# Context feed-forward placed right behind the last expert's scatter, gate products moved to a later stage, three start orders changed

## The chip, the cores and the metric

One core of a Trainium2 chip runs the whole program, one launch. The metric is device time in microseconds from the start to the end of that launch; the profile is one further execution, taken by the hardware profiler, whose rows are in microseconds from its first instruction.

## What is computed

Two transformer blocks in float32 over 256 tokens of width 1024, cut here to what the change touches.

```python
x = x + mix @ w_out[0]; x = x + swiglu(rmsnorm(x, g), wg, wu, wd)        # layer 0: dense, 3584 wide
x = x + attention(rmsnorm(x, attn_norm[1])) ...                          # layer 1
x = x + moe_swiglu(rmsnorm(x, g), router, ...)                           # 8 experts, top 2 of them per token
x = rmsnorm(x, final_norm)
# second block; modulation vectors from silu(c) @ w_ada, for x and for a context of 256 tokens
xs = ffn_half(x, ...);  cs = ffn_half(ctx, ...)                          # the same weights, 2816 wide
#   ffn_half: s + 0.5 * gate * rmsnorm(swiglu(modulate(rmsnorm(s), shift, scale)), g_post)
xs = xs + mod * rmsnorm(token_mixer(...)); xs = ffn_half(xs, ...)        # last: ff1
```

## The kernel before

Each engine has an order of its own, written out by hand in one function per engine (SyncE for loads, TensorE, GpSimd, ScalarE, VectorE); semaphores tie them. There is no planner. A name such as `rows_high` (ScalarE) and `rows_low` (VectorE) is the same step's part on each engine.

**Products of split numbers.** A float32 matrix is split in a high part (ScalarE copies it with rounding, `..._high`) and a low part (VectorE subtracts the high part from the original, `..._low`). A product is three products: high by high, high by low, low by high. A block of weights is 1024 by 512, loaded in two halves of 1 MB into `ringA` (two blocks deep), and split half by half into `As`, which has one buffer (`A_parts` L2258, `unit_high`, `unit_low`), or for projections into `ringH`/`As` and `ringL` (`weight_high` L1573, `weight_low` L2226). Down weights go through `ringB` into `Bs`. SyncE reloads a half of `ringA` in a feed-forward when its low part is made, in a projection when TensorE has used it.

**A feed-forward** (`feed`, L783 for TensorE, L1610 ACT, L2268 DVE) runs over blocks of 256 hidden columns, for two tiles of 128 tokens. Per block TensorE does gate and up products with the first weight half (24), turns the hidden values of the block before, does 24 with the second half, then the block before's 24 down products. ScalarE does per block: hidden high part, As half, silu of two tiles, As half, Bs; VectorE the low parts of these and the product of gate and up. The hooks `before`, `after`, `turns_free` put other work at the start or the end of a given block. ff0c is the context's feed-forward, ff0x that of x with the same weights behind it; 11 blocks each.

**The experts** (`expert`, L965 PE, L1737 ACT, L2378 DVE) work on at most 128 gathered rows, so one tile: 14 blocks each of 12 + 12 + 12 products, with the gather of the next expert's rows in block 12 and the scatter of the one before's result (`keep_y`, `y_low`, `scatter` L952, `add` L2367) in blocks 2 and 3. The last expert ends with its own order in the last block: an alternative home for the down weights (`down_home`), then three products of the identity that nothing reads (`idle_products` L701), then its two scatters, each followed by VectorE's add to x through the same two accumulator banks 6 and 7.

**Behind the experts**, before: VectorE signals x; ScalarE and VectorE split the context rows `hcT` into `xs` (`x_parts`); ScalarE takes the squares of x, VectorE scales it with the final norm, ScalarE takes each tile's statistics for ff0x's norm and VectorE scales into `xn` (L1937 to L1943, L2735 to L2746); then ff0c's loop starts. Its hooks turn the rows of ff0x (`x_rows`) in blocks 1 to 3 and split them into `hcTR` and `hTR`.

**The second attention's start** (L1788 ff., L2503 ff.): two weight halves are split, the dense result is added tile by tile (`settle`), each tile is normed (`tile_stats`, `tile_root`, `tile_scale`), turned by TensorE (`turn_rows`), and split (`rows_high`, `rows_low`).

**GpSimd** (L1469) does two things: it finishes the modulation columns, and after the last modulation row it forms four gate rows (L1487 to L1500) of 128 by 1024, with six loads of 0.5 MB on its own queue. The first reader of these is the end of ff0c (`post`, in ff0x's first block).

**ff1's start** (L2968 ff.): VectorE makes both As halves, then for tile 0 `mixed_out`, `mixed_add`, `tile_scale`, and so on.

Of the kernel before, what the change touches and what calls it, by code (L numbers as in the profile page):

```python
# [28 lines left out]
P = 128  # L29
SEQ = 256  # L30
D = 1024
# [101 lines left out]
def build(nc, t, out, AT1, N1, AT2, N2):  # L133
    ctx = ExitStack()
    with ctx:
# [14 lines left out]
        hcT = sb("hcT", [P, KC, SEQ])  # L150
        xn = sb("xn", [P, TILES, D])
# [113 lines left out]
        split_h = [hcTR, hTR]  # L265
        Kc, Vc = gateG[:, 0:2, :], cs
# [149 lines left out]
        for nm in ("attn0", "mix0", "ffn0", "attn1", "mix1", "ffn1", "ff0x", "ff1"):  # L416
            mixed, plain = nm[:3] == "mix", nm in ("ffn1", "ff0x")
            PN[nm] = dict(at, mixed=mixed, plain=plain)
            for key, add_ in (("std", 2), ("xn", 4 if mixed else 2), ("tp", 4), ("hi", 2 if plain else 4), ("lo", 2 if plain else 4)):
                at[key] += add_  # L420

# [275 lines left out]
        def _(pe):  # L697
# [24 lines left out]
            def turn_rows(nm, tt, hf):  # L722
# [3 lines left out]
                for j in range(4):  # L726
                    last = tr(ps[:, rows_bank(nm, tt, hf), j * P:(j + 1) * P], xn[:, tt, (4 * hf + j) * P:(4 * hf + j + 1) * P], ident)
# [224 lines left out]
            def scatter(e, tt):  # L952
# [5 lines left out]
                if tt or isinstance(e, int) and e == NE - 1:  # L958
                    pe.wait_ge(added, 2 * e + tt)
                for half in range(2):  # L960
                    for q in range(2):
                        last = mm(ps[:, 6 + half, :], selT[:, tt, :], ye[q][:, half * 512:(half + 1) * 512], start=q == 0, stop=q == 1)
# [176 lines left out]
            for l in range(2):  # L1139
# [17 lines left out]
                if l == 0:  # L1157
                    feed(ph["dense"], split_stream, 2, rows="ffn0")
            def logits(tt):
# [26 lines left out]
            with pe.If(pe.value_load(most[0:1, 0:1], min_val=0, max_val=SEQ) < CAP + 1):  # L1186
# [5 lines left out]
                idle_products(3)  # L1192
# [12 lines left out]
            def x_rows_out(n):  # L1205

                if n in (2, 3):
                    pe.wait_ge(pn_hi, PN["ff0x"]["hi"] + n - 1)
                    pe.wait_ge(pn_lo, PN["ff0x"]["lo"] + n - 1)
            feed(ph["ff0c"], split_stream, 2, ready=2 * ph["ff0c"]["xc"] + 1, xsm=xs_split, head=2, drains=False, after=x_rows, turns_free=x_rows_out)  # L1210
            feed(ph["ff0x"], lambda l, tt, k: split_h[l][:, k, tt * P:(tt + 1) * P], 2, ready=2 * ph["ff0x"]["xc"] + 1, xsm=xs_split, leads=False)
# [258 lines left out]
        def _(pool):  # L1470
# [16 lines left out]
            pool.wait_ge(spread_copied, units_before(NADA))  # L1487
            for w, (gain, bias, rows_, fac) in enumerate(((1, 2, (0, 1), 0.5), (3, 5, (2,), 1.0), (5, 8, (3,), 0.5))):
# [15 lines left out]
        def _(act):  # L1504
# [39 lines left out]
            def tile_stats(nm, tt, src, wait, cols=None, j=None):  # L1544
# [5 lines left out]
                ch.done(A(xn[:, tt, sl], src[:, tt, sl], ACT.Square, accum_out=ss[:, j:j + 1]))  # L1550
# [174 lines left out]

            def rows_part(e, h):
# [10 lines left out]
            def expert(e):  # L1737
# [3 lines left out]
                def before(n):  # L1741
                    if n == 2 and not first:
                        keep_y(e - 1)

                def body(i, u, last):
# [4 lines left out]
                    if not lead:  # L1750
                        part_high(e, i - 1, u, 1)
                    unit_high(e, *nxt, 0)
# [7 lines left out]
                    if last and final:  # L1760
# [1286 lines left out]
```

## Time and profile before

| | us |
|---|---|
| three runs | 2671.5, 2678.55, 2677.37 |
| their median | 2677.37 |
| the profiled execution's own time | 2677.7 |
| its span, first to last instruction | 2675.9 |
| PE busy (mean granted clock 0.975 of full speed) | 2551.6 |
| DVE busy | 1824.0 |
| ACT busy | 1452.0 |
| POOL busy | 57.5 |

PE is TensorE, DVE VectorE, ACT ScalarE, POOL GpSimd, SP SyncE (SPq its queue of loads). A row of a timeline has start, duration of the group, engine, line, operation, tiles written and read, shape and count; in brackets how long the engine was idle before it and what ended that. A PE matmul row's duration includes the pipeline's drain, so starts are better compared than ends. The chain of waits is the work that ended last, followed back from the end; its rows have start, duration, engine, tile written, line and count.

### The profile page before, as it was taken

Reading aid. Unit: us, or ns where it says so; the run is one execution under the profiler, and the core shown is the slowest. Engines: PE = TensorE matmul, PEld = TensorE weight load, DVE = VectorE, ACT = ScalarE, POOL = GpSimd, SP = SyncE. Lnnn points to the kernel's source line nnn. Section 1 sums busy time; section 2 is a strip of 40 time slices with the busy share of each in tenths; the row PEclk is TensorE's granted clock in tenths of the full one; section 3 lists DMA queues with packets and bytes.
Section 4 is the critical chain, followed back from the end, with each engine's and each line's share of the span. In section 5 each row is a group of like instructions: output and inputs, shape, how many; then the busy total and the mean of one; then the engine's idle time right before and its main releaser. Section 6 shows DMA issues by size and latency. Waiting matters only on the chain.

```text
span 2675.9 us, 33561 instructions
## 1 busy us (share of the span) xinstructions
PE 2551.6 (95%) x11949; PEld 2028.0 (76%) x11949; DVE 1824.0 (68%) x1779; ACT 1452.0 (54%) x1613; POOL 57.5 (2%) x40
## 2 busy tenths in 40 slices
PE   7899998888999999999999998999999999998998
PEld 6578887666878787888888886888884687776787
DVE  6554555559898989888888886555443475776544
ACT  4554434545777777777777675445432343465443
POOL 0000000016000000000000000000000000000000
PEclk9989998889999999999999998999999999999999
DMA  6865542758999999999999996556543344435552
GB/s 216 294 215 186 184 169 79 252 181 328 356 348 349 353 342 358 348 351 349 353 340 361 332 345 217 180 182 194 181 166 108 99 148 119 137 100 175 195 185 70
DMA packets 327742, 631.65 MB, mean 236 GB/s; under 512 B 14088, under 2 KB 112936, under 8 KB 327464
## 3 DMA queue, kind: packets, MB, share of 16 engines
q1 hardware_dynamic: 326792, 627.35, 67.5%
q0 software_dynamic: 864, 3.15, 0.3%
q8 instruction: 55, 0.90, 0.1%
q14 instruction: 31, 0.25, 0.0%
HBM read 629.40 MB, written 1.05 MB: 236 GB/s over the span
## 4 chain that ended last, share of the span: by engine, by line
PE 84%; DVE 8%; ACT 4%; issue 3%; DMA 1%; SPq 0%; DVEq 0%; ACTq 0%
PE ps L894 18%; PE ps L820 18%; PE ps L924 11%; PE ps L849 9%; PE ps L1289 6%; PE ps L754 5%; PE ps L1316 2%; PE ps L1221 2%; DVE As L2261 2%; PE ps L1027 1%; PE ps L949 1%; ACT As L1679 1%; PE ps L833 1%; PE ps L909 1%; PE ps L1280 1%
## 5 line engine op out<-in xcount | busy, mean ns | idle before, releaser
L2261 DVE TENSOR_TENSOR As<-ringA,As 128x2048 fp32r<-128x2048 f32 x318 | 737.8, 2322 | 220.2 <-ACT As L1598 127.5
L894 PE MATMUL ps<-As,xgs 128*128 128x512 f32 x2688 | 660.9, 395 | 10.5 <-DVE As L2261 7.8
L894 PEld LDWEIGHTS ps<-As,xgs 128*128 128x128 f32 x2688 | 494.9, 188 | 117.6 <-DVE As L2261 6.8
L1679 ACT ACTIVATE As<-ringA 128x2048 fp32r<-128x2048 f32 x224 | 428.7, 1914 | 29.9 <-PE ps L894 28.1
L820 PE MATMUL ps<-As,xs 128*128 128x512 f32 x1632 | 391.5, 396 | 9.3 <-DVE xs L2199 5.3
L820 PEld LDWEIGHTS ps<-As,xs 128*128 128x128 f32 x1632 | 305.8, 189 | 76.1 <-issue 5.7
L924 PE MATMUL ps<-Bs,hds 128*128 128x512 f32 x1332 | 324.6, 393 | 13.7 <-DVE hds L2322 13.5
L924 PEld LDWEIGHTS ps<-Bs,hds 128*128 128x128 f32 x1332 | 250.0, 189 | 72.5 <-issue 19.3
L2341 DVE TENSOR_TENSOR Bs<-ringB,Bs 128x2048 fp32r<-128x2048 f32 x111 | 260.4, 2346 | 11.0 <-ACT Bs L1709 9.5
L1709 ACT ACTIVATE Bs<-ringB 128x2048 fp32r<-128x2048 f32 x111 | 213.1, 1920 | 74.8 <-PE ps L924 74.8
L849 PE MATMUL ps<-Bs,hds 128*128 128x512 f32 x1056 | 247.8, 390 | 0.0
L849 PEld LDWEIGHTS ps<-Bs,hds 128*128 128x128 f32 x1056 | 198.0, 188 | 41.9
L1598 ACT ACTIVATE As<-ringA 128x2048 fp32r<-128x2048 f32 x94 | 179.8, 1913 | 16.7 <-DMA ringA<-in_dense_w_up 9.7
L2305 DVE TENSOR_TENSOR Bs<-ringB,Bs 128x2048 fp32r<-128x2048 f32 x44 | 100.9, 2293 | 119.7 <-ACT Bs L1652 119.7
L1652 ACT ACTIVATE Bs<-ringB 128x2048 fp32r<-128x2048 f32 x44 | 84.3, 1916 | 135.4 <-PE ps L849 135.4
L2231 DVE TENSOR_TENSOR ringL<-ringA,ringH 128x2048 fp32r<-128x2048 f32 x42 | 96.1, 2290 | 57.3 <-ACT ringH L1578 57.1
L1689 ACT ACTIVATE hds<-ps 128x256 fp32r<-128x256 f32 x112 | 43.0, 384 | 156.2 <-PE ps L909 155.5
L754 PE MATMUL ps<-As,xs 128*128 128x512 f32 (+1 forms) x384 | 119.0, 393 | 8.6 <-DVE ringL L2231 5.7
L1619 ACT ACTIVATE hds<-ps 128x256 fp32r<-128x256 f32 x94 | 31.3, 382 | 171.1 <-PE ps L833 163.1
L1578 ACT ACTIVATE ringH<-ringA 128x2048 fp32r<-128x2048 f32 x42 | 80.1, 1911 | 79.1 <-PE ps L1289 57.6
L820 PE MATMUL ps<-As,hcTR 128*128 128x512 f32 x352 | 111.6, 398 | 0.0
L1640 ACT ACTIVATE sg<-ps 128x256 f32<-128x256 f32 x94 | 36.0, 383 | 126.1 <-PE ps L820 125.1
(380 smaller groups left out, 3210.2 us busy)
## 6 DMA issues: line engine op xcount, KB each, us to landing
ringA<-in_moe_w_gate SPq DMA_DIRECT2D x112, 1024.0 KB, 5.1
ringA<-in_moe_w_up SPq DMA_DIRECT2D x112, 1024.0 KB, 5.7
ringB<-in_moe_w_down SPq DMA_DIRECT2D x112, 1024.0 KB, 5.5
ringA<-in_w_ff_in SPq DMA_DIRECT2D x132, 512.0 KB, 4.8
ringA<-in_w_in SPq DMA_DIRECT2D x56, 1024.0 KB, 5.4
ringA<-in_w_ada SPq DMA_DIRECT2D x36, 1024.0 KB, 6.2
ringB<-in_w_ff_out SPq DMA_DIRECT2D x33, 1024.0 KB, 5.0
ringA<-in_dense_w_gate SPq DMA_DIRECT2D x28, 512.0 KB, 3.6
```

The lines of the kernel that those rows point to most:

```text
L754: m = mm(ps[:, 4 + 2 * (n % 2) + tt, 0:cols], xs[:, l, k, tt * P:(tt + 1) * P], w, start=k == 0 and m_ == 0, stop=k == KC - 1 and m_ == 2)
L820: m = mm(ps[:, bank, :], lhs(l, tt, k), As[:, h, r, k % 4, :], start=k == 0 and n == 0, stop=k == KC - 1 and n == 2)
L849: m = mm(ps[:, 4 + 2 * tt + half, :], hds[:, buf, l, q, :], w[:, half * 512:(half + 1) * 512], start=first and q == 0 and n == 0, stop=q = ...
L894: m = mm(ps[:, bank, :], lhs(l, tt, k), As[:, h, r, k % 4, :], start=k == 0 and n == 0, stop=k == KC - 1 and n == 2)
L924: m = mm(ps[:, 4 + 2 * tt + half, :], hds[:, u if T == 1 else tt, l, q, :], (Bs[:, q, r, :] if weights is None else weights[r][:, q, :])[: ...
L1289: m = mm(dst, lhs[l][:, k, tt * P:(tt + 1) * P], w[q], start=k == 0 and m_ == 0, stop=k == KC - 1 and m_ == 2)
L1598: A(As[:, h, 0, :, :], ringA[:, (p["a"] + u) % 2, 4 * h:4 * h + 4, :], ACT.Copy).then_inc(A_high, 1)
L1679: A(As[:, h, 0, :, :], ringA[:, (p["a"] + u) % 2, 4 * h:4 * h + 4, :], ACT.Copy).then_inc(A_high, 1)
L1709: A(Bs[:, :, 0, :] if dst is None else dst, ringB[:, b0 % 2, :, :], ACT.Copy).then_inc(B_high, 1)
L2261: V.tensor_tensor(As[:, h, 1, :, :], ringA[:, (p["a"] + u) % 2, 4 * h:4 * h + 4, :], f32(As[:, h, 0, :, :]), ALU.subtract).then_inc(A_spli ...
L2305: V.tensor_tensor(Bs[:, :, 1, :], ringB[:, (p["b"] + u) % 2, :, :], f32(Bs[:, :, 0, :]), ALU.subtract).then_inc(B_low, 1)
L2341: V.tensor_tensor(lo, ringB[:, (p["b"] + u) % 2, :, :], f32(hi), ALU.subtract).then_inc(B_low, 1)
```

## The change

1. The gate rows on GpSimd wait until the second of ff0x's row turns is through (`pn_lo`), in ff0c's third block.
2. The context rows are split in blocks 0 and 1 of the last expert, into `xn` and `hcTR` (`context_high`, `context_low`), once its own gather has read `xn`.
3. The last expert's last block has a new order on ACT and DVE: down weights and the product of gate and up before ff0c's first As halves, the second of which comes after the accumulator is saved. The two scatters use banks 6, 7 and 2, 3, so the second does not wait for the first one's add; two idle products instead of three.
4. The squares of x, its final norm and ff0x's statistics move into ff0c: on ACT to the start of block 1, ahead of the hidden parts, with a table load behind; on DVE to the end of block 0. They use an area of the arena (`x_tok`) instead of `xn`; `tokens(nm)` gives that area to the helpers `tile_stats`, `tile_scale` and `turn_rows`. ff0x's rows are split into `xs` and `hTR` (`split_x`).
5. Two idle products behind the dense feed-forward; at the second attention's start DVE adds tile 0 before its first weight half and makes the second half after tile 0's rows; ACT copies the second half after tile 0's root and turns to tile 1's square after tile 0's rows.
6. At ff1's start DVE makes the second As half after tile 0's add.

The diff, cut; the numbers are lines of the kernel before, indentation is one blank per level, `xnR` is `xn` seen as rounded numbers.

```diff
@@ -263 @@
   split_h = [hcTR, hTR]
+  split_c = [xnR[:, :, :].rearrange("p t n -> p (t n)").rearrange("p (k n) -> p k n", k=KC), hcTR]
+  split_x = [xs[:, 1, :, :], hTR]
+  x_tok = ar(0, TILES, D)
@@ -418 @@
+  def tokens(nm):
...
+   return x_tok if nm == "ff0x" else xn[:, :, :]
@@ -955 @@
       pe.wait_ge(xg_ready, 2 * e + 4)
-    if tt or isinstance(e, int) and e == NE - 1:
+    final = isinstance(e, int) and e == NE - 1
+    if final != bool(tt):
      pe.wait_ge(added, 2 * e + tt)
+    bank = 2 if final and tt else 6
...
      for q in range(2):
-      last = mm(ps[:, 6 + half, :], selT[:, tt, :], ye[q][:, half * 512:(half + 1) * 512], start=q == 0, stop=q == 1)
+      last = mm(ps[:, bank + half, :], selT[:, tt, :], ye[q][:, half * 512:(half + 1) * 512], start=q == 0, stop=q == 1)
@@ -1156 @@
      feed(ph["dense"], split_stream, 2, rows="ffn0")
+     idle_products(2)
@@ -1189 @@
     expert(NE - 1)
-    idle_products(3)
+    idle_products(2)
@@ -1204 @@
+    if n == 1:
+     pe.wait_ge(x_ready, XR["moe"])
...
      pe.wait_ge(pn_lo, PN["ff0x"]["lo"] + n - 1)
-   feed(ph["ff0c"], split_stream, 2, ready=2 * ph["ff0c"]["xc"] + 1, xsm=xs_split, head=2, drains=False, after=x_rows, turns_free=x_rows_out)
-   feed(ph["ff0x"], lambda l, tt, k: split_h[l][:, k, tt * P:(tt + 1) * P], 2, ready=2 * ph["ff0x"]["xc"] + 1, xsm=xs_split, leads=False)
+   feed(ph["ff0c"], lambda l, tt, k: split_c[l][:, k, tt * P:(tt + 1) * P], 2, ready=2 * ph["ff0c"]["xc"] + 1, xsm=xs_split, head=2, drains=False, after=x_rows, turns_free=x_rows_out)
+   feed(ph["ff0x"], lambda l, tt, k: split_x[l][:, k, tt * P:(tt + 1) * P], 2, ready=2 * ph["ff0x"]["xc"] + 1, xsm=xs_split, leads=False)
@@ -1485 @@
    pool.wait_ge(spread_copied, units_before(NADA))
+   pool.wait_ge(pn_lo, PN["ff0x"]["lo"] + 2)
@@ -1723 @@
+   def context_high(h):
...
+    act.wait_ge(nt_act, 4 * (call["ff0c"] + 1))
+    act.wait_ge(nt_dve, 4 * (call["ff0c"] + 1))
+    A(split_c[0][:, 4 * h:4 * h + 4, :], hcT[:, 4 * h:4 * h + 4, :], ACT.Copy).then_inc(xs_high, 1)
@@ -1739 @@
     def before(n):
+     if n == 0 and final:
+      act.wait_ge(gathered, 2 * NE)
+     if n in (0, 1) and final:
+      context_high(n)
@@ -1749 @@
       part_high(e, i - 1, u, 1)
+     if last and final:
+      down_high(e, i, 0, down_home(ph["moe"], ph["moe"]["b"])[0], 0)
+      unit_high(e, *nxt, 0)
+      part_high(e, i, 0, 1)
+      part_high(e, i, 1, 1, 3)
+      down_high(e, i, 1, None, 2)
+      unit_high(e, *nxt, 1)
+      return
@@ -1757 @@
       rows_part(e + 1, 1)
-     if last and final:
-      down_high(e, i, 0, down_home(ph["moe"], ph["moe"]["b"])[0], 0)
-      part_high(e, i, 0, 1)
-      part_high(e, i, 1, 1, 3)
-      down_high(e, i, 1, None, 2)
-     elif u:
+     if u:
@@ -1795 @@
      act.wait_ge(tile_done, p["td"])
-     for h in range(2):
-      weight_high(p, 0, h)
+     weight_high(p, 0, 0)
...
      tile_root(tt, tt + 1, D)
-     if tt == 0 or l == 0:
-      continue
-     for hf in range(2):
-      rows_high(f"attn{l}", 0, hf, col(8 * l))
+     if l and tt == 0:
+      weight_high(p, 0, 1)
+      for hf in range(2):
+       rows_high(f"attn{l}", 0, hf, col(8 * l))
@@ -1934 @@
     all_tokens(NE - 1)
-   act.wait_ge(x_ready, XR["moe"])
-   x_parts(hcT, call["ff0c"])
...
-   squares(lambda tt: x[:, tt, :], 1, 1e-5)
-   for tt in range(TILES):
-    tile_stats("ff0x", tt, x, [(x_ready, XR["final"])])
-    tile_root(tt, tt + 1, D, 1e-6)
+    for h in range(2):
+     context_high(h)
@@ -1949 @@
+    if n == 1:
+     act.wait_ge(x_ready, XR["moe"])
+     squares(lambda tt: x[:, tt, :], 1, 1e-5, lambda tt, q: x_tok[:, tt, :])
+     for tt in range(TILES):
+      tile_stats("ff0x", tt, x, [(x_ready, XR["final"])])
+      tile_root(tt, tt + 1, D, 1e-6)
+     nc.scalar.preload_act_table(ACT.Silu)
@@ -1960 @@
      for h in range(2):
-      A(hcTR[:, 4 * h:4 * h + 4, :], hT[:, 4 * h:4 * h + 4, :], ACT.Copy).then_inc(xs_high, 1)
+      A(split_x[0][:, 4 * h:4 * h + 4, :], hT[:, 4 * h:4 * h + 4, :], ACT.Copy).then_inc(xs_high, 1)
@@ -2367 @@
     dve.wait_ge(mixed_back, 2 * e + (tt + 1))
-    V.tensor_tensor(x[:, tt, :], x[:, tt, :], ps[:, 6:8, :].rearrange("p a b -> p (a b)"), ALU.add).then_inc(added, 1)
+    b = 2 if tt and isinstance(e, int) and e == NE - 1 else 6
+    V.tensor_tensor(x[:, tt, :], x[:, tt, :], ps[:, b:b + 2, :].rearrange("p a b -> p (a b)"), ALU.add).then_inc(added, 1)
@@ -2380 @@
     def after(n):
+     if n in (0, 1) and final:
+      context_low(n)
@@ -2401 @@
       part_low(e, i - 1, u, 1)
+     if last and final:
+      gate_times_up(e, i, 1)
+      down_low(e, i, 0, down_home(ph["moe"], ph["moe"]["b"]))
+      part_low(e, i, 0, 1)
+      part_low(e, i, 1, 1, 3)
+      down_low(e, i, 1)
+      unit_low(e, *nxt, 0)
+      y_low(e)
+      unit_low(e, *nxt, 1)
+      return
@@ -2409 @@
       rows_part(e + 1, 1)
-     if last and final:
-      down_low(e, i, 0, down_home(ph["moe"], ph["moe"]["b"]))
-      part_low(e, i, 0, 1)
-      part_low(e, i, 1, 1, 3)
-      down_low(e, i, 1)
-     elif u:
+     if u:
@@ -2422 @@
     if final:
-     y_low(e)
...
+   def context_low(h):
...
+    dve.wait_ge(xs_high, 2 * ph["ff0c"]["xc"] + h + 1)
+    V.tensor_tensor(hcTR[:, 4 * h:4 * h + 4, :], hcT[:, 4 * h:4 * h + 4, :], f32(split_c[0][:, 4 * h:4 * h + 4, :]), ALU.subtract).then_inc(xs_split, 1)
@@ -2508 @@
     else:
+     settle(0)
      weight_low(p, 0, 0)
-     settle(0)
-     weight_low(p, 0, 1)
...
       rows_low(attn, 0, hf, col(8 * l))
+     weight_low(p, 0, 1)
@@ -2732 @@
     dve.wait_ge(acc_free, 1 + NE)
+    for h in range(2):
+     context_low(h)
    dve.sem_inc(x_ready, 1)
-   x_parts(hcT, ph["ff0c"]["xc"])
...
-   dve.wait_ge(nrm_std, SQ["final"])
-   ch.done(V.reciprocal(rr[:, 0:2], std[:, 0:2]))
-   for tt in range(TILES):
-    last = V.scalar_tensor_tensor(x[:, tt, :], x[:, tt, :], rr[:, tt:tt + 1], fnrow[:, :], ALU.mult, ALU.mult)
-   last.then_inc(x_ready, 1)
-   dve.wait_ge(x_ready, XR["final"])
-   for tt in range(TILES):
-    tile_scale("ff0x", tt, x, tt + 1)
...
+    if n == 0:
+     dve.wait_ge(nrm_std, SQ["final"])
+     ch.done(V.reciprocal(rr[:, 0:2], std[:, 0:2]))
+     for tt in range(TILES):
+      last = V.scalar_tensor_tensor(x[:, tt, :], x[:, tt, :], rr[:, tt:tt + 1], fnrow[:, :], ALU.mult, ALU.mult)
+     last.then_inc(x_ready, 1)
+     dve.wait_ge(x_ready, XR["final"])
+     for tt in range(TILES):
+      tile_scale("ff0x", tt, x, tt + 1)
@@ -2755 @@
       dve.wait_ge(xs_high, 2 * ph["ff0x"]["xc"] + h + 1)
-      V.tensor_tensor(hTR[:, 4 * h:4 * h + 4, :], hT[:, 4 * h:4 * h + 4, :], f32(hcTR[:, 4 * h:4 * h + 4, :]), ALU.subtract).then_inc(xs_split, 1)
+      V.tensor_tensor(hTR[:, 4 * h:4 * h + 4, :], hT[:, 4 * h:4 * h + 4, :], f32(split_x[0][:, 4 * h:4 * h + 4, :]), ALU.subtract).then_inc(xs_split, 1)
@@ -2968 @@
     weight_low(p, 1, h)
-   for h in range(2):
-    A_parts(ph["ff1"], 0, 0, 0, h)
+   A_parts(ph["ff1"], 0, 0, 0, 0)
@@ -3002 @@
    mixed_add(0)
+   A_parts(ph["ff1"], 0, 0, 0, 1)
```

## Rows read from the trace of the kernel before

**Rows 1.** The page, part 4: shares of the chain that ended last.

```profile
PE 84%; DVE 8%; ACT 4%; issue 3%; DMA 1%; SPq 0%; DVEq 0%; ACTq 0%
```

**Rows 2.** Windows: length, busy PE, PEld, DVE, ACT, POOL (counts), PEclk, DMA share, GB/s.

```profile
594.00:724.00 130.00, 115.53 (x513) 92.90 (x512) 113.53 (x68) 82.33 (x60) 46.30 (x18) 0.97 0.93 340
724.00:850.00 126.00, 124.44 (x574) 101.84 (x573) 111.52 (x81) 89.71 (x67) 0.00 (x0) 1.00 0.97 350
1670.00:1740.00 70.00, 70.00 (x324) 57.86 (x322) 38.28 (x38) 33.04 (x39) 0.00 (x0) 1.00 0.56 181
```

**Rows 3.** The chain from 408 to 428 us: start, us, engine, tile, line, count.

```profile
410.10 2.30 DVE ringL L2231
415.84 0.75 DVE xn L2207
417.75 1.16 ACT xn L1550 x2
419.23 1.04 ACT xs L1563 x4
420.29 1.14 DVE xs L2223 x4
421.56 5.46 PE ps L754 x12
427.02 1.30 PE ps L727 x8
```

**Rows 4.** First expert: timeline of POOL and DVE, then PE's waits from 594 to 665.

```profile
601.48 7.32 POOL L1493 TENSOR_TENSOR gateG<-gateG,arow 128x1024 f32<-128x1024 f32 x2 [5.21 <-DMA arow<-in_b_ada]
602.08 8.88 DVE L2261 TENSOR_TENSOR As<-ringA,As 128x2048 fp32r<-128x2048 f32 x2
609.71 7.35 POOL L1496 TENSOR_SCALAR gateG<-gateG 128x1024 f32<-128x1024 f32 x2
612.14 2.29 DVE L2261 TENSOR_TENSOR As<-ringA,As 128x2048 fp32r<-128x2048 f32 x1 [1.19 <-ACT As L1679]
...
PE ps L894 <- DVE As L2261: 7.8, 6, 2.1
PE ps L924 <- DVE hds L2322: 5.1, 3, 3.0
```

**Rows 5.** Experts to ff0c: page part 6, timeline, and two chain rows.

```profile
ringB<-in_moe_w_down SPq DMA_DIRECT2D x112, 1024.0 KB, 5.5
...
1610.10 0.37 SPq L604 DMA_DIRECT2D ringB<-in_moe_w_down  x1
...
1617.28 1.90 ACT L1709 ACTIVATE Bs<-ringB 128x2048 fp32r<-128x2048 f32 x1
...
1619.74 1.22 PE L924 MATMUL ps<-hTR,hds 128*128 128x512 f32 x2 [2.86 <-DVE hds L2322]
...
1638.58 1.04 ACT L1514 ACTIVATE xn<-x 128x1024 f32<-128x1024 f32 x1
...
1639.95 12.37 PE L820 MATMUL ps<-As,xs 128*128 128x512 f32 x47 [5.32 <-DVE xs L2199]
...
1640.91 1.28 ACT L1515 ACT_TABLE_LOAD   x1
...
1647.81 0.30 ACT L1554 ACTIVATE std<-ss,small 128x1 f32<-128x1 f32 x1
...
1628.34 2.58 PE ps L704 x6
...
1664.35 5.46 PE ps L849 x24
```

**Rows 6.** A middle expert's block 2, timeline of PE.

```profile
884.56 3.01 PE L924 MATMUL ps<-Bs,hds 128*128 128x512 f32 x12 [0.28 <-DVE hds L2322]
```

**Rows 7.** Groups by form, PE: 1700 to 1784 (ff0c), 1840 to 1925 (ff0x).

```profile
L820 PE MATMUL ps<-As,xs 128*128 128x512 f32 x240 | 57.1, 394 | 0.0
...
L820 PE MATMUL ps<-As,hcTR 128*128 128x512 f32 x160 | 50.7, 398 | 0.0
```

More of the change, by code:

```diff
@@ L150, in build @@
         hcT = sb("hcT", [P, KC, SEQ])
+        with nc.sbuf_tensor("xnR", [P, TILES, D], F32R) as xnR:
+            pass
         xn = sb("xn", [P, TILES, D])
@@ L726, in turn_rows @@
                 for j in range(4):
-                    last = tr(ps[:, rows_bank(nm, tt, hf), j * P:(j + 1) * P], xn[:, tt, (4 * hf + j) * P:(4 * hf + j + 1) * P], ident)
+                    last = tr(ps[:, rows_bank(nm, tt, hf), j * P:(j + 1) * P], tokens(nm)[:, tt, (4 * hf + j) * P:(4 * hf + j + 1) * P], ident)
                 last.then_inc(pn_tp, 1)
@@ L1549, in tile_stats @@
                 sl = slice(0, D) if cols is None else cols
-                ch.done(A(xn[:, tt, sl], src[:, tt, sl], ACT.Square, accum_out=ss[:, j:j + 1]))
+                ch.done(A(tokens(nm)[:, tt, sl], src[:, tt, sl], ACT.Square, accum_out=ss[:, j:j + 1]))
             def tile_root(j0, j1, n, eps=1e-5):
@@ L2206, in tile_scale @@
                 ch.done(V.reciprocal(rr[:, j:j + 1], std[:, j:j + 1]))
-                V.tensor_scalar(xn[:, tt, sl], src[:, tt, sl], rr[:, j:j + 1], None, ALU.mult).then_inc(pn_xn, 1)
+                V.tensor_scalar(tokens(nm)[:, tt, sl], src[:, tt, sl], rr[:, j:j + 1], None, ALU.mult).then_inc(pn_xn, 1)
             def rows_low(nm, tt, hf, scale):
```

## The prediction

> **What bounds the kernel now.** I read the page's chain first: of the work that ended last TensorE (PE) holds 84%, VectorE (DVE) 8% and ScalarE (ACT) 4% [rows 1]. So time is won only where PE stands idle or runs at 1.2 GHz. The windows say where that is [rows 2]: in the first expert PE is idle 130.0 - 115.5 = 14.5 us at a granted clock of 0.97, in the next one 1.6 us at 1.00; in the context feed-forward (ff0c) PE is busy 70.0 of 70.0 us with DVE at 38.3. The change touches four seams (dense to second attention, first expert, experts to ff0c, start of ff1), and I step through each with the durations of the rows. The sum is made against the profiled execution's own 2677.7 us (span 2675.9), 0.3 us above the median of the runs shown, 2677.37.
>
> **1. Start of the second attention: 5.5 us earlier.** The chain before [rows 3] runs: ACT copies a half weight, DVE subtracts it (410.10, 2.30), only then adds the dense result, subtracts the second half, scales tile 0; ACT does tile 1's square (417.75) before tile 0's rows (419.23, 1.04), DVE their low half (1.14), and PE starts at 421.56. After: DVE adds tile 0 while ACT copies, so ACT squares at about 410.3 and DVE subtracts one half meanwhile, 410.3 to 412.6. Scaling takes 0.75 and 0.2 around it: 413.5. Half the transposes 0.7, ACT 1.04, DVE 1.14: first product at 416.7, 4.9 earlier. PE then wants tile 1: DVE finishes tile 0's other rows (417.7), the moved subtraction (2.30, 420.0) and the scale (0.9): transposes at 421.0 in place of 427.02, 6.0 earlier. The two idle products are 0.9 each by the three of [rows 5] (2.58 for x6): they fill 411.9 to 413.7, just before the transposes, and cost at most 0.2. The twelve products that took 5.46 (1.2 GHz; 24 warm ones take 5.46 too, [rows 5]) may stay at 2.4 GHz, as the gaps are then under 2 us; if not, they end at 422.2 and the gain is 4.8. I take 5.5, ends 3 and 6.5. Weight loads of this seam are issued when PE frees a half and shift with it.
>
> **2. Gate products out of the first expert: 11 us.** POOL works 46.3 us there [rows 2]. While it runs a two-input product (601.48) two DVE subtractions take 8.88 together, against 2.29 each otherwise, 4.3 more; beside its one-input product (609.71) one takes 2.29 [rows 4]. PE waits 7.8 us for As subtractions and 5.1 for hidden ones there, 12.9 of its 14.5 idle. Part of that stays: with 2.29 a subtraction, 1.9 a copy and 2.75 for twelve products [rows 5], the one As buffer leaves waits of 1.5, 0.6, 0.8 and 0.1 in the first two blocks, and the one-hots about 1.0 in block 3: 4.0 in all. The low clock goes too, 3% of 130 us is 3.9 us of full speed, of which I count 2 because PE was idle for the rest. 12.9 - 4.0 + 2 = 11. Ends: 8 (clock gives nothing and a wait is left), 13.
>
> The products now follow the second turn of ff0x's rows, so POOL and its six 0.5 MB loads lie in ff0c. DVE is busy 38.3 of 70 us there and PE never waits [rows 2]; even the 4.3 of a pair is under the 7.7 us that DVE has free in each block of 16.9 (three groups of 24 products at 5.5 and a turn). Cost 0, other end 3. Their reader, the end of ff0c, is over 100 us later. Without that cover the cost is rival 3.
>
> A rule speaks against this. The rows: DVE at 2.29 beside POOL's one-input product. The Trainium skill, "SBUF — State Buffer", section on SBUF's two sides, says that VectorE with two SBUF inputs and GpSimd take the shared port pair for a whole instruction and the loser blocks. The two-input rows agree, the one-input row does not. By that rule every subtraction in ff0c could wait for one POOL instruction (3.7 us) and the sum would be 11.4 in place of 23.4, a time of 2666; by the row it is 2654.
>
> **3. Experts to ff0c: 8.4 us earlier.** Before [rows 5]: PE waits 2.86 and starts the last two blocks' down products at 1619.74 at the low clock; three idle products (2.58); scatter, add, scatter; x split into xs; 5.32 idle; ff0c from 1639.95. After, step by step. Two As subtractions (2 x 2.29) leave DVE's queue ahead of the down weights: down starts at 1615.1. Twelve products, 1617.8. The last down block's copy started at 1617.28 behind ACT's other work; its load was issued at 1610.1 and takes 5 to 5.5, so about 1615.4; a copy of 1.9 and a subtraction of 2.3 later PE goes on at 1619.7, done 1622.4. Accumulator copied (1.1, like the square of that size) and subtracted (1.2, half of 2.29), with handovers 2.5; two scatters without the add between (own banks), 1.9: 1626.9. The context rows are split already, so ff0c's first product is there, 13 us earlier; its second As half is due at 1632.4 and ready at 1627.2. 48 products: 1637.9; 24, turn, 24: 1649.4. Now the new wait: ACT, once its Bs copy ends (1642.2), does the final norm's squares and ff0x's statistics before the hidden copies. That stretch ran from 1638.58 to 1648.11 [rows 5], and a table load of 1.28 more makes it 10.8: 1653.0, hidden parts 0.9, down products at 1653.9 in place of 1664.35: 10.4 earlier. Behind ACT's stretch stand its As and Bs copies, which PE reaches later than they need. The 4.5 idle lowers the clock, as 5.32 did (47 products in 12.37 in place of 10.8): minus 2.0. 8.4. Ends 5 and 11. DVE's part of that norm lies inside the stretch.
>
> **4. Context split in the last expert: 2.0 us lost.** DVE is busy 111.5 of 126 [rows 2] and gets two more subtractions of half size (1.2 each by the 2.29 one) in blocks 0 and 1. ACT has room. DVE's slack is 14.5 of 126, about 1.0 a block; behind the second stand the y subtraction and the hidden one that PE already waited 0.28 for at that place [rows 6]: 2.4 + 0.28 less the 0.7 that blocks 0 and 1 can absorb beside their own unevenness gives 2.0, ends 0.5 and 3.
>
> **5. Operands.** ff0c reads xn and hcTR in place of xs, ff0x reads xs and hTR in place of hcTR and hTR. A product is 394 ns from xs, 398 from hcTR [rows 7]; 528 products in each stage at 4 ns are 2.1 us, lost in one and won in the other: 0, ends -2 and +2.
>
> **6. ff1: 0.5 us.** The second As subtraction (2.29, [rows 4]) stood before tile 0's mix and now stands after its add, beside ACT's square; it delays the scale by 0.8 of the 1.4 that it frees. Loads wait for that half but SP is still issuing others.
>
> Sum: 5.5 + 11 + 8.4 - 2.0 + 0 + 0.5 = 23.4; 2677.7 - 23.4 = 2654.
>
> **Rivals.** *Forecast*, 0.64: about 2654, own range 2647 to 2661.
> *1, the final norm eats the seam*, 0.14: ACT's stretch in ff0c's second block grows to twice its 10.8 less what PE has to do meanwhile, and PE goes slow for longer; item 3 gives 1 to 2: 2661. For it: a chain over ACT and DVE in the middle of PE work. Against: its parts lasted 9.5 together.
> *2, the first expert is paced by loads*, 0.08: that window moved 340 GB/s at a share of 0.93, the next 350 at 0.97 [rows 2]. The same bytes in 119 us want 371. At 355 the window would need 124.5: item 2 gives 5.5: 2660. Against: no wait of PE's there leads back to a load.
> *3, the gate products cost as much in ff0c*, 0.08: three subtractions a block, each behind a 3.7 us POOL instruction, take 18 us, with DVE's smaller parts about 20.6, 3.7 over a block's 16.9; POOL's 46.3 us of work last for three to four blocks: 12 us back, 2666. It is the port rule of the Trainium skill's "SBUF — State Buffer" told above.
> *4, slower*, 0.03: ff0c's stationary halves lie in two tensors (xn, hcTR) and each of its 528 products loses time in the weight load. To end over 2677.4 + 8 it must take 31 us, 59 ns a product on 229. The rows know 4 ns, hence the small chance; anything under 44 ns still ends below before.
> *5, it does not do what it says*, 0.03: ff0c's first product still waits as it did, since the gathered path is not what decides but the late As half, and rivals 2 or 3 come along: 2670 to 2677.
>
> **How the numbers follow.** 2654 is the forecast case. The range of 2646 to 2665 takes nearly all of it and rivals 1 and 2; it leaves out about 2 in 10. A measurement of this kernel can tell about 0.3% (8 us) from no change. Faster by more: the forecast, rivals 1 and 2 and half of 3, 0.90. Within: the other half of 3 and rival 5, 0.07. Slower: rival 4, 0.03.
>
> **What would show it.** Right: no POOL row near 600 and As subtractions of 2.29 there; the second gather 11 us earlier relative to the first; POOL's rows some 35 us after ff0c's start with PE busy throughout; first attention product 5 us after the dense stage's last one and not 10; two scatters back to back, ff0c's products directly behind; one new wait of 4 to 5 us of PE's down products for hidden parts in ff0c's second block. Wrong: waits of PE for As or hds in ff0c's blocks 3 to 6 (rival 3), DMA as a releaser in the first expert (rival 2), a wait over 8 us in ff0c's second block (rival 1), a mean over 400 ns for ff0c's products (rival 4), or a wait over 3 us in the last expert's third block (item 4).

## The result and the profile after

| | before | after |
|---|---|---|
| median of the runs | 2677.96 (4 runs, 2671.5 to 2682.1) | 2656.01 (4 runs, 2654.8 to 2659.7) |
| the profiled execution | 2677.7 | 2659.7 |
| its span | 2675.9 | 2657.9 |
| PE busy, mean granted clock | 2551.6, 0.975 | 2548.6, 0.978 |

The ratio is 0.9918 with a 95% interval of 0.9895 to 0.9942: 22 us by the medians. The profiled execution of after is 3.7 above its median, so the two traces differ by 18.0 only. The change was run once more under the name after_again: 2657.17 (6 runs), span 2657.7.

The chain of the page of after, beside [rows 1]: PE gains a point, DVE loses one.

```profile
PE 85%; DVE 7%; ACT 4%; issue 3%; DMA 1%; SPq 0%; DVEq 0%; ACTq 0%
```

**A ledger by stages** comes from the starts of the same PE work in each trace; what is left over between two such marks is the stage's own. Gathers are the eight `ps<-arena,xn` groups; a turn in this table is a group of transposes of hidden values, `ps<-c,hh`.

| from, to (us) | before | after | item |
|---|---|---|---|
| dense's last down group to the attention's last projection | 64.2 | 57.9 | 1 |
| to the first gather | 118.9 | 117.2 | |
| first to second gather | 128.3 | 116.4 | 2 |
| second to last gather | 757.7 | 757.7 | |
| last gather to the last expert's first scatter | 150.5 | 146.3 | 3, 4 |
| to ff0c's first product | 9.1 | 3.9 | 3 |
| to ff0c's first down products | 24.2 | 28.7 | 3 |
| to the turn in ff0c's block 2 | 11.8 | 14.8 | 3 |
| to ff0x's last turn | 332.8 | 334.0 | 5 |
| to ff1's first turn | 490.1 | 492.3 | 6 |

Windows of after, columns as in [rows 2]: the first expert has no POOL, the next is as it was, and ff0c now carries POOL for 43.3 us with PE still busy all the time. POOL's first product starts 67 us behind ff0c's first one (1678.36 against 1611.25), where the prediction had said some 35.

```profile
587.00:703.00 116.00, 110.92 (x499) 90.35 (x498) 95.20 (x67) 81.11 (x59) 0.00 (x0) 0.98 0.94 346
703.00:829.00 126.00, 124.49 (x574) 101.90 (x573) 111.82 (x80) 89.66 (x66) 0.00 (x0) 1.00 0.98 353
1670.00:1740.00 70.00, 70.00 (x313) 57.00 (x312) 44.58 (x35) 29.71 (x30) 43.26 (x18) 1.00 0.71 226
```

The chain of after at the second attention's start, beside [rows 3]: the dense stage's end, the idle products (L713), tile 0's turn, rows, and the first products at 417.15.

```profile
404.12 8.26 PE ps L858 x36
412.39 1.72 PE ps L713 x4
...
417.15 4.51 PE ps L763 x12
421.67 0.87 PE ps L736 x8
```

Experts to ff0c, beside [rows 5]. Timeline of PE and ACT of after, with the idle time ahead in brackets.

```profile
1601.81 2.97 PE L933 MATMUL ps<-Bs,hds 128*128 128x512 f32 x12 [1.44 <-DVE Bs L2370]
1607.30 0.50 PE L973 MATMUL ps<-arenaR 128*128 128x512 f32 x1 [0.81 <-DVE hTR L2478]
1609.03 0.39 PE L973 MATMUL ps<-hTR,arenaR 128*128 128x512 f32 x1
1611.25 0.82 PE L829 MATMUL ps<-As,xnR 128*128 128x512 f32 x2 [1.83 <-issue]
1618.73 1.92 ACT L1613 ACTIVATE As<-ringA 128x2048 fp32r<-128x2048 f32 x1 [12.80 <-PE ps L829]
1628.17 1.04 ACT L1529 ACTIVATE arena<-x 128x1024 f32<-128x1024 f32 x1
1634.84 1.06 ACT L1565 ACTIVATE arena<-x 128x1024 f32<-128x1024 f32 x1 [2.75 <-DVE x L2786]
1638.99 0.66 ACT L1634 ACTIVATE hds<-ps 128x256 fp32r<-128x256 f32 x2
1639.94 8.46 PE L858 MATMUL ps<-Bs,hds 128*128 128x512 f32 x24 [4.07 <-issue]
```

The scatters are back to back and ff0c starts 2.2 us behind the last of them. Its first down products wait 4.07 us: their releaser reads "issue", but ACT's hidden copies end at 1639.65 and DVE's low parts follow, and ahead of them on ACT stands the norm from 1628.17 to 1638.98. The trace also shows a hole that the prediction had not seen: ACT idle for 12.80 us up to 1618.73, right where x is complete.

### The profile page after: what moved, and what is told of

Read it like the earlier page. It is cut to its first block, busy times and chain, and to the rows that moved or that the text cites. A ratio compares the mean times of both kernels' runs of the same rounds, so it can differ in the third digit from the quotient of the medians.

```text
span 2657.9 us, 33567 instructions
## 1 busy us (share of the span) xinstructions
PE 2548.6 (96%) x11951; PEld 2023.4 (76%) x11951; DVE 1814.3 (68%) x1779; ACT 1452.1 (55%) x1613; POOL 54.4 (2%) x40
## 4 chain that ended last, share of the span: by engine, by line
PE 85%; DVE 7%; ACT 4%; issue 3%; DMA 1%; SPq 0%; DVEq 0%; ACTq 0%
PE ps L829 19%; PE ps L903 19%; PE ps L933 11%; PE ps L858 10%; PE ps L1303 6%; PE ps L763 5%; PE ps L1330 2%; PE ps L1235 1%; DVE As L2290 1%; PE ps L1038 1%; PE ps L958 1%; PE ps L918 1%; PE ps L842 1%; ACT Bs L1724 1%; ACT As L1694 1%
## 5 line engine op out<-in xcount | busy, mean ns | idle before, releaser
L829 PE MATMUL ps<-As,xs 128*128 128x512 f32 x1456 | 376.1, 396 | 3.9 <-DVE hh L2325 3.9
L933 PE MATMUL ps<-Bs,hds 128*128 128x512 f32 x1332 | 322.4, 391 | 11.8 <-DVE hds L2351 9.0
L829 PEld LDWEIGHTS ps<-As,xs 128*128 128x128 f32 x1456 | 271.9, 189 | 63.3 <-DVE hh L2325 4.8
L2370 DVE TENSOR_TENSOR Bs<-ringB,Bs 128x2048 fp32r<-128x2048 f32 x111 | 254.1, 2290 | 12.4 <-ACT Bs L1724 10.8
L1613 ACT ACTIVATE As<-ringA 128x2048 fp32r<-128x2048 f32 x94 | 179.8, 1913 | 29.1 <-PE ps L829 12.8
L829 PE MATMUL ps<-As,xnR 128*128 128x512 f32 x352 | 112.8, 402 | 1.8 <-issue 1.8
```

The lines of the kernel that those rows point to most:

```text
L829: m = mm(ps[:, bank, :], lhs(l, tt, k), As[:, h, r, k % 4, :], start=k == 0 and n == 0, stop=k == KC - 1 and n == 2)
L933: m = mm(ps[:, 4 + 2 * tt + half, :], hds[:, u if T == 1 else tt, l, q, :], (Bs[:, q, r, :] if weights is None else weights[r][:, q, :])[: ...
L1613: A(As[:, h, 0, :, :], ringA[:, (p["a"] + u) % 2, 4 * h:4 * h + 4, :], ACT.Copy).then_inc(A_high, 1)
L2370: V.tensor_tensor(lo, ringB[:, (p["b"] + u) % 2, :, :], f32(hi), ALU.subtract).then_inc(B_low, 1)
```

## The experiments

Medians below stand beside 2656 to 2657 for the changed kernel. A single trace says less than it seems to: with the same code ahead of it, the dense stage's last down group starts anywhere from 406.6 to 411.9 us. So stages are compared, and a stage with its clock beside it.

**1. The gate products alone**, on the kernel before.

```diff
     pool.wait_ge(spread_copied, units_before(NADA))
+    pool.wait_ge(pn_lo, PN["ff0x"]["lo"] + 2)
```

> The kernel before with one edit: the four gate rows on POOL wait for the second of ff0x's row turns. The traces of before and after put the two gathers around the first expert 128.1 and 116.2 us apart, 11.9 less. Theory (POOL's two-input products slow the subtractions there, and they cost nothing in ff0c): 11 to 12 us under before, the same 11.9 between the gathers, and DVE subtractions of 4 us and more beside POOL's two-input rows in ff0c with no wait of PE's behind them. Rival (the change's other edits made the first expert shorter, its starting clock above all): under 6 us. Rival (they cost as much in ff0c): within 2 us of before.

Measured: 2665.74 (6 runs) against 2679.06, ratio 0.9943 (0.9923 to 0.9964). Gather to gather 114.9 in place of 128.3, 13.4 less; from the turn in block 2 to ff0x's last one 332.8 as before, so in ff0c the products cost nothing. The theory holds. 1.5 more than 11.9 is the clock of the first gather: its products lead to the first expert's own in 5.7 us here, and in 7.2 in before and in after.

**2. The gate products back**, in the changed kernel (the same line taken out).

> The changed kernel with the gate rows back in the first expert. Theory: 11 to 12 us over the changed kernel, all of it between the first two gathers (116.2 back to 128). Rival (they cost 3 us or more in ff0c): the first expert loses 12, and ff0c from its 25th product on gets 3 or more shorter, 9 or less over the changed kernel.

Measured: 2673.16 (12 runs), 17 over the changed kernel, and 134.1 between the gathers: 17.6 lost, not 11.9. From ff0c's block 2 on it is 334.0 as in after, so rival 3 is out to the hundredth. The same work costs 11.9 to 13.4 in one timing and 17.6 in another. Between the gathers PE stands idle 17.2 us here, 14.5 in before and 5.1 in after; the rest of the difference to before is clock, granted at 0.93 here and at 0.97 in before. PE's waits here, from 586 to 721, against 7.8 and 5.1 of [rows 4]:

```profile
PE ps L903 <- DVE As L2289: 10.3, 5, 4.1
PE ps L933 <- DVE hds L2350: 5.5, 1, 5.5
```

**3. Gate products of one input**, in the first expert.

```diff
-     ch.done(G.tensor_tensor(gateG[:, g, :], gateG[:, g, :], vec_row, ALU.add))
+     ch.done(G.tensor_scalar(gateG[:, g, :], gateG[:, g, :], 0.5, None, ALU.mult))
```

and the same for the product with the gain.

> The changed kernel with the gate rows back in the first expert, and every product and sum of two tiles on POOL there put in as a product of one tile and a constant, so the gate rows are not the reference's: the same six loads and 12 instructions of 128 by 1024 on POOL, none with two inputs. The first two gathers lie 116.4 us apart without POOL's work and 134.1 with it. Theory (it is POOL's two-input instructions that hold up DVE's subtractions): DVE's subtractions stay at 2.3 us beside POOL, 116.4 to 118 between the gathers. Rival (any POOL instruction blocks DVE's two-input ones for as long as it runs, the port rule): the POOL work is as long or longer, so 134 or more. Rival (the six loads of 0.5 MB in the way of the weights): 120 or more with DVE at 2.3.

Measured: 2660.78 (5 runs); 119.4 between the gathers, 2.9 over no POOL work and 14.7 under two-input work. The window shows POOL as busy as with two inputs (44.2 us), and the first instructions of DVE beside it:

```profile
593.32 6.42 POOL L1507 TENSOR_SCALAR gateG<-gateG 128x1024 f32<-128x1024 f32 x2 [5.25 <-DMA arow<-in_b_ada]
594.82 2.28 DVE L2289 TENSOR_TENSOR As<-ringA,As 128x2048 fp32r<-128x2048 f32 x1
598.46 2.29 DVE L2289 TENSOR_TENSOR As<-ringA,As 128x2048 fp32r<-128x2048 f32 x1 [1.36 <-ACT As L1693]
```

In the run with two inputs the same two came out as one pair of 7.48:

```profile
593.19 5.15 POOL L1507 TENSOR_TENSOR gateG<-gateG,arow 128x1024 f32<-128x1024 f32 x2 [5.16 <-DMA arow<-in_b_ada]
596.05 7.48 DVE L2289 TENSOR_TENSOR As<-ringA,As 128x2048 fp32r<-128x2048 f32 x2
```

DVE's mean As subtraction from 586 to 660 is 2.46 us against 3.09, with 2.29 undisturbed. Of the sixteen subtractions of 128 by 2048 that overlap a one-input row eleven took 2.3 and five 3.0 to 3.45, the longest this one beside the POOL row at 651.28:

```profile
651.28 2.79 POOL L1510 TENSOR_SCALAR gateG<-gateG 128x1024 f32<-128x1024 f32 x1
651.03 5.66 DVE L2289 TENSOR_TENSOR As<-ringA,As 128x2048 fp32r<-128x2048 f32 x2
```

(its pair is 3.45 and 2.28). So it is mostly the two-input instructions; a small price, 2.9 us, is left, and whether the loads or those longer rows make it stays open. By the port rule of the Trainium skill's "SBUF — State Buffer" every one of POOL's instructions would have held DVE's; the rows agree for two inputs and not for one. Nor are one-input rows free of DVE: POOL's own took 2.79 us at best and up to 4.43 beside it.

**4. The second attention's start back** in the changed kernel (the orders of ACT and DVE as before, no idle products).

> The changed kernel with the start of the second attention as before: both weight halves ahead, no idle products behind the dense feed-forward. Theory: 6.3 us lost up to the seam's end and the heads' 1.6 with it, so 6 to 8 over the changed kernel, PE's first attention product 10 us behind the dense feed-forward. Rival (the 1.6 in the heads was chance): 6.3 at the seam and nothing more behind it.

Measured: 2663.48 (6 runs), 7 over by the medians and 10.0 by the trace. To the last projection it is 63.6 against 57.9, 5.7 of it; the other 4.3 arises in the heads. The granted clock of the 30 us behind the projection goes with it (windows of after, then of this run):

```profile
469.30:499.30 30.00, 26.46 (x214) 16.70 (x213) 19.36 (x38) 14.63 (x51) 0.00 (x0) 1.00 0.86 297
```

```profile
475.07:505.07 30.00, 26.83 (x182) 16.45 (x184) 17.82 (x33) 13.60 (x47) 0.00 (x0) 0.83 0.77 266
```

Dense's last down group to the first gather took 175.1 to 176.2 us in ten of eleven traces with the new order and 183.1, 185.2 and 185.0 in the three with the old one. The eleventh, of experiment 6, has the new order, took 179.5, and has a clock of 0.83 there. So the theory's 6.3 + 1.6 is not what happens: the same code behind the seam runs at one of several clocks, 0.83, 0.94 or 1.00, and two of these came with either order. With the old order it never had the best, but that is three traces, and whether the order bears on it is not shown.

**5. No idle products behind dense.**

```diff
-     idle_products(2)
```

> The changed kernel without the two idle products behind the dense feed-forward. They were to keep PE at 2.4 GHz for the first attention products and did not: the first eight or so of twelve still ran at 1.2. Theory (they do nothing here): the transposes behind them and the first attention product, 5.39 us after the dense stage's last down group, come within 0.3 us of that, and the twelve products take the same 4.5. Rival (they did keep a part of the clock): the eight transposes take 2 us in place of 1.1 and the twelve products 5.3, 1 to 2 us later on.

Measured (one run, 2654.68): the first attention product 5.38 behind the last down group, against 5.39, at the same cold start:

```profile
408.82 1.09 PE L736 MATMUL ps<-c,xn 128*128 128x128 f32 x8 [1.62 <-DVE xn L2235]
411.96 0.76 PE L763 MATMUL ps<-As,xs 128*128 128x512 f32 x1 [2.05 <-DVE xs L2251]
```

The idle products do nothing here: with them and without them PE stands 2.05 us ahead of the first attention product and runs at 1.2 GHz for 3.4 us from there on.

**6. The norm in the hole.** On ACT the squares before block 0, the statistics behind its first As half; on DVE the scaling of x before the loop.

```diff
-    if n == 1:
+    if n == 0:
      act.wait_ge(x_ready, XR["moe"])
      squares(lambda tt: x[:, tt, :], 1, 1e-5, lambda tt, q: x_tok[:, tt, :])
...
+   def x_stats(n):
...
+   feed(ph["ff0c"], 2, ahead=True, head=2, drains=False, before=x_rows, mid=x_stats)
```

> The changed kernel with the final norm taken out of ACT's way: the squares of x and their root at the very start of ff0c, where ACT's trace is idle for 12.8 us and DVE's for 8.9; DVE scales x at once; ACT's statistics for ff0x follow its first As half in block 0, DVE's scaling of the rows its own. Theory (PE's 4.07 us before ff0c's first down products is ACT's norm ahead of the hidden copies, and the 24 products of 8.46 us after it are slow for that wait): the wait is gone, the 24 products take 5.5, 7 us under the changed kernel. Rival (the copies of block 0 come late instead, As for the next block or the first silu): a new wait of 1 to 4 us at the next As half and a gain of 3 or less. Rival (the wait has another cause, as PE's down weights): it stays, no change.

Measured: 2651.94 (6 runs), ratio 0.9898 (0.9880 to 0.9916). From ff0c's first product to its first down products 25.2 in place of 28.7, from there to block 2's turn 12.0 in place of 14.8: 6.3 less. The wait and the slow products after it are gone together, so the cause is ACT's norm. The size needs a range: seven other traces with after's code from ff0c on take 40.7 to 42.7 us for the two stretches together, against 43.5 in after and after_again, 37.1 here, so 3.6 to 6.3 less. A small part of the first rival is there too, silu behind the statistics:

```profile
PE ps L829 <- DVE hh L2333: 1.4, 1, 1.4
```

**7. The norm split.** Squares at the start with the scaling, the statistics in block 1 again.

```diff
-    if n == 1:
+    if n == 0:
      act.wait_ge(x_ready, XR["moe"])
      squares(lambda tt: x[:, tt, :], 1, 1e-5, lambda tt, q: x_tok[:, tt, :])
+    if n == 1:
      for tt in range(TILES):
...
+   feed(ph["ff0c"], ..., before=x_rows, mid=lambda n: nc.scalar.preload_act_table(ACT.Silu) if n == 0 else None)
```

> The changed kernel with only the squares of x and their root at the start of ff0c on ACT, DVE's scaling with the final norm right behind, ACT's silu table again behind its first As half; ACT's statistics for ff0x stay ahead of the hidden copies of block 1, DVE's scaling of the rows at the end of block 0. In the run that moved all of it, PE waited 1.4 us for the product of gate and up, whose silu stood behind the statistics. Theory (each piece fits in a gap of its own): ACT's stretch in block 1 is 5.5 us in place of 9.5 and starts at the same place, so the hidden parts are there 0.6 us before PE wants them and neither the 4.07 nor the 1.4 wait is left; 8 us under the changed kernel. Rival (the stretch in block 1 with its two table loads is still too long): a wait of 1 us or more before the first down products and no more than the 6.6 us that the whole move gave.

Measured: 2651.99 (6 runs, 2648.03 to 2656.65), profiled span 2646.2. 23.2 and 12.0 for the two stretches, 8.3 less than after and 5.5 to 7.6 less than the seven others: both waits are gone. Of the 11.7 us between the spans of this trace and after's, 5.1 lie ahead of the first seam, where the code is the same. Its PE waits and the down products:

```profile
1606.15 0.70 PE L829 MATMUL ps<-As,xnR 128*128 128x512 f32 x2 [1.60 <-issue]
1629.36 2.91 PE L858 MATMUL ps<-Bs,hds 128*128 128x512 f32 x12
1631.66 3.35 PE L858 MATMUL ps<-Bs,hds 128*128 128x512 f32 x14
```

The medians differ by 5.2 from after_again, at the lower end of that range, with ratios to before of 0.9916 (0.9900 to 0.9931) and 0.9929 (0.9915 to 0.9943): the stage is shown in the trace, its size in whole runs is not settled.

**8. Idle products behind the branch.**

```diff
      all_tokens(NE - 1)
+   idle_products(8)
```

> The changed kernel with eight idle products (some 1.9 us) right behind the branch that ends the experts on PE. PE stands 1.83 us between the last scatter product and ff0c's first one, with its operands ready. Theory (it is the way out of the branch): the gap of 1.8 stays ahead of the idle products, and ff0c's first product comes 1.9 later behind them. Rival (ff0c's first product waits for something that the profile does not show): the idle products follow the scatter at once and fill the gap, ff0c's first product stays where it was.

Measured (one run, 2661.35): the gap stays ahead of the idle products.

```profile
1609.26 7.13 PE L713 MATMUL ps<-c 128*128 128x512 f32 x16 [1.74 <-issue]
1615.83 1.03 PE L829 MATMUL ps<-As,xnR 128*128 128x512 f32 x2
```

They wait for no semaphore, so the 1.7 us is not a wait of ff0c's for its operands but belongs to leaving the branch, as the theory has it. The packets of the instruction queue say more: in all fourteen traces a load of 16 KB of instructions lands 1.4 to 1.5 us before PE issues its first instruction behind the branch. In after it runs from 1608.54 to 1609.72, with PE's next instruction at 1611.14; where it lands later behind the last scatter, the gap is longer, from 1.5 us up to 2.1. In before it runs from 1637.31 to 1638.44, with PE's next instruction at 1639.84, and xs's first half was ready at 1638.99, so the wait of 5.32 that [rows 5] puts down to xs may have ended by this load instead. That the load is the cause is read from these times alone; no run was made to move it.

The eight products took 7.1 us, not 1.9, and at full clock:

```profile
1609.30:1616.00 6.70, 6.70 (x17) 3.10 (x17) 0.64 (x1) 0.00 (x0) 0.00 (x0) 1.00 0.87 307
```

This window of PE, PEld, DVE, ACT and POOL has a granted clock of 1.00. One idle product is two instructions of 0.43 us each, as the three of [rows 5] were (2.58 for x6); eight are 6.9 by that row, so the expectation's 1.9 was mispriced. ff0c came 6.5 later behind the scatter. The way from its first product to its first down products, 27.5 us, is 1.2 shorter than in after, but five other traces without idle products take 27.2 to 27.8 as well: it is the clock of ff0c's start, not these products.

**9. One more DVE instruction ahead of each context half.**

```diff
+      ch.done(V.tensor_tensor(hcT[:, 4 * h:4 * h + 4, :], hcT[:, 4 * h:4 * h + 4, :], hcT[:, 4 * h:4 * h + 4, :], ALU.max))
```

> The changed kernel with one more DVE instruction of two inputs and 128 by 1024 ahead of each half of the context split in the last expert's blocks 0 and 1 (the larger of a tile and itself, which leaves it as it is). The context split moved the last expert's last block by 1.5 us. Theory (DVE has almost no slack in blocks 0 and 1, PE waits for what stands behind): the last gather and the first scatter, 146.3 us apart, come to lie 1.5 to 2.5 further apart. Rival (the 1.5 is the late start of the split, a wait for ACT's copies): under 0.5 more.

Measured (one run, 2657.38): 148.9 from the last gather to the first scatter, 2.6 more, as much as the two instructions themselves (1.2 each) and a little over. PE's waits for hidden low parts go from 0.7 to 1.9 and for hTR from 1.4 to 2.6. Blocks 0 and 1 have no slack left.

**10. Context half in block 12**, on top of the split norm.

```diff
-     if n in (0, 1) and final:
-      context_high(n)
+     if n in (0, NB1 - 2) and final:
+      context_high(min(n, 1))
```

and the same for `context_low`.

> The version with the split norm, and the second half of the context split moved from the last expert's block 1 to its block 12, where the other experts make the next one's one-hots and this one makes none. Theory (each block has some 0.8 us of DVE to spare; blocks 0 to 3 of the last expert each carry 1.2 more, 0.4 too much each, 1.6 in all; block 12 has room): the last gather and the first scatter come 0.4 to 1.0 closer than 146.3 us. Rival (the last block is what is late, for DVE's chain there): no change or up to 1 us more. ff0c as in the version with the split norm: 23.2 us from its first product to its first down products, 12.0 from there to the second turn if the clock stays up; 5 to 9 us under the changed kernel's 2656.

Measured: 2649.26 (6 runs, 2645.62 to 2657.16), ratio 0.9892 (0.9871 to 0.9912). The stage takes 146.1, only 0.2 less than in after, where traces with after's code spread from 146.3 to 146.9: a miss. ff0c took 24.1 and 12.0 for its two stretches, near the 23.2 and 12.0 expected. The wait of 1.4 for hTR in block 3 is gone, but in the last block the wait for Bs is 2.0 in place of 1.4 and that for hidden parts 0.6 in place of 0.3, and 0.3 of idle time is new elsewhere, so what blocks 0 to 3 won was lost at the other end. It is clearly faster than before; its 2.7 under experiment 7 are no more than such runs spread.

**11. ff1's order back.**

```diff
-   A_parts(ph["ff1"], 0, 0, 0, 0)
+   for h in range(2):
+    A_parts(ph["ff1"], 0, 0, 0, h)
```

> The changed kernel with ff1's first two As halves together again. Theory: the way from the last mixer product to ff1's first turn is 0.7 us longer and nothing else moves; below what the times of whole runs can tell. Rival (the loads behind the half matter): 2 us or more, either way.

Measured: 2656.34 (6 runs), no difference. From the last mixer product to ff1's first transposes 4.04 us, against 3.50 and 3.73 in the two traces of after: 0.3 to 0.5. Over all traces it is 4.03 to 4.20 in the three with the old order and 3.38 to 3.73 in the eleven with the new one.

## Why the prediction was right, point by point

**1, second attention: 5.5 said; 5.7 to 6.3 up to the last projection, and 1.7 to 4.3 more in the heads.** The first product came 4.9 closer to the dense stage (10.31 to 5.39), just as worked out, and the eight transposes for tile 1 at 421.67, 5.8 earlier than before relative to that stage. But the twelve products did not stay at 2.4 GHz: they took 4.51, half of them slow, and experiment 5 shows that the idle products have no part in it. The prediction's ground for a clock that stays up, gaps under 2 us, did not hold: the gap ahead of the first product was 2.05. A clock in the heads that differs from run to run stood in no step, so the 1.7 won there is luck.

**2, first expert: 11 said; 11.9 in the traces, 13.4 alone.** Cost in ff0c 0 said, and 0.0 in experiments 1 and 2. The waits that were to remain, 4.0, are 3.0 (As), 1.5 (rows) and 0.6 (hidden), 5.1 of idle time in all. None of them leads back to a load, and experiment 3 moved 365 GB/s in this window at 119.4 us, so rival 2 is out; its estimate also kept the six gate loads, 3 MB, which leave with the products. In ff0c DVE's subtractions beside POOL's two-input rows took up to 4.5 us as they had done in the first expert, and PE did not notice, as DVE had a third of the time free:

```profile
1703.48 2.39 POOL L1508 TENSOR_TENSOR gateG<-gateG,arow 128x1024 f32<-128x1024 f32 x1 [3.79 <-DMA arow<-in_b_ada]
1703.48 4.54 DVE L2334 TENSOR_TENSOR Bs<-ringB,Bs 128x2048 fp32r<-128x2048 f32 x1 [2.85 <-ACT Bs L1667]
1684.41 6.92 POOL L1511 TENSOR_SCALAR gateG<-gateG 128x1024 f32<-128x1024 f32 x2
1686.39 2.30 DVE L2334 TENSOR_TENSOR Bs<-ringB,Bs 128x2048 fp32r<-128x2048 f32 x1 [0.74 <-ACT Bs L1667]
```

**3, experts to ff0c: 8.4 said, 3.4 measured in after's trace, up to 6 in others; this is the term that was mis-sized.** Entering the last block after is 17.9 ahead of before, and at the turn in block 2 21.3. The steps held up to the scatters: the last block's down products at 1601.81 (1619.7 in before's time, as said), the last scatter product at 1609.03. The first product of ff0c was said to be 13 earlier and was 10.8: 1.83 us went to the way out of the branch, which had lain inside a wait of 5.32, and 0.4 to handovers. ff0c then started at 1.2 GHz (granted clock 0.79 from 1611 to 1619, 1.00 after), which cost 1.4 us by experiment 7, whose first products take 23.2 with no wait (28.7 - 4.07 - 23.2). That start is not the kernel's own: six traces with the same code have 1.00 there and take 27.2 to 27.8 in place of 28.7. ACT's stretch took 10.82 (10.8 said), but it stands behind block 0's silu and two copies, and these follow PE's 48th product; as that came late by the late and slow start, the stretch began 3.9 later than said, at 1628.17, and the down products came 6.4 earlier in place of 10.4. The slow products behind the wait cost 3.0, not 2.0 (the prediction's own row, 12.37 in place of 10.8, gives 1.6). 6.4 less 3.0 is the 3.4. From the first scatter to block 2's turn after takes 47.4 us and the traces with the same code there 44.9 to 47.5, so with the better clock the item is worth up to 6. The wait itself, 4.5 said, was 4.07: rival 1's norm was there at forecast size.

**4, context split: 2.0 said, 1.5 measured** (19.4 ahead at the last gather, 17.9 at the last block). Experiment 9 confirms the kind, DVE without slack; experiment 10 shows that moving a half gives back only 0.2, so a sum of slacks by blocks is too simple.

**5, operands: 0 said, 1.2 lost.** Products of ff0c take 398 ns from xn and 396 from hcTR against 394 [rows 7]; from block 2 to ff0x's first turn that is 1.7 us. ff0x won only 0.45 back, since products from xs took 399 ns there, not 394.

```profile
L829 PE MATMUL ps<-As,xnR 128*128 128x512 f32 x160 | 50.7, 398 | 0.0
L829 PE MATMUL ps<-As,hcTR 128*128 128x512 f32 x80 | 31.7, 396 | 0.0
```

```profile
L829 PE MATMUL ps<-As,xs 128*128 128x512 f32 x160 | 50.8, 399 | 0.0
L829 PE MATMUL ps<-As,hTR 128*128 128x512 f32 x80 | 31.4, 393 | 0.0
```

So it is not the tensor's name that sets the rate. What does was not tried.

**6, ff1: 0.5 said, 0.3 to 0.5.**

**The sum.** 6.3 + 1.7 + 11.9 + 3.4 - 1.5 - 1.2 + 0.5 is 21.1; the traces differ by 18.0, as 0.5 was lost ahead of the first seam and 2.6 in the stage between ff0x and ff1. That stage has the code of before but for ff1's order, and took 490.4 to 495.4 in the runs of the experiments against 490.1 in before's trace, so what is lost there is within what that stage spreads, though before's trace has the least of all. 2654 was said for 2656; the 5 missing in item 3 were for the most part made up by items 1, 2 and 4 and the heads. The number owes its closeness in part to that.

## What to carry to other kernels

A step taken off an engine's way is only as good as the place it goes to: look for the hole in each engine's own trace once the wait in front is gone, for here 12.8 us of idle ACT ended 9.4 us ahead of the place chosen. A wait that is removed uncovers what it hid (the way out of a branch, a cold clock), so price the next thing behind it. And an engine with a third of its time free takes a doubled instruction without cost, where one at 88% passes nearly all of it on. Last, a stretch of one trace can owe its clock to chance: before a difference of 2 us is given a cause, look at the same code in every other trace.

## What the runs showed of the hardware

- A DVE two-input instruction of 2.29 us that starts while POOL runs a two-input one of 128 by 1024 takes up to 4.5. Where DVE's starts first it keeps its 2.3, and POOL's takes up to 4.5 in place of 2.4 (experiment 2: DVE 2.28 at 629.39, POOL 4.41 at 629.51). Beside a one-input one DVE's stays at 2.3 in eleven of sixteen cases and takes 3.45 at worst.
- Leaving the branch leaves PE idle for 1.5 to 2.1 us in the twelve traces in which nothing else holds it, and the next instruction comes 1.4 to 1.5 us behind the landing of a 16 KB load of instructions in all fourteen.
- The granted clock behind the second attention's projection was 1.00, 0.94 or 0.83 over 30 us with the same code, worth up to 4.4 us (175.1 against 179.5).
- An idle product, plain float32 and 512 columns wide, is two instructions of 0.43 us each at a granted clock of 1.00; one product of rounded parts of that width takes 0.23 there. Eight of them held ff0c back by 6.5 us.
